# Encoder trunk on one Trainium2 core: the gate's norm divided between two engines, the attention sums copied one step sooner, and a narrower final norm

## The chip, the cores and the metric

The kernel runs on 1 core of one Trainium2 chip. The metric is the device time of one execution, in microseconds (us), smaller is better. The core has five engines that run their own instruction streams and meet at semaphores: TensorE (PE; its weight loads are shown as PEld), VectorE (DVE), ScalarE (ACT), GpSimd (POOL) and SyncE (SP, which here only issues transfers).

## The reference

An encoder of 2 layers over 512 positions of width 1024, all in float32. Each layer has a mixer of two kinds of heads side by side, a cross-attention into 256 memory tokens, and a gated MLP with a convolution of width 3. The change touches the mixer and the final norm. Cut to these:

```python
def rmsnorm(x, g):
    return x * rsqrt(mean(x * x, -1) + EPS) * g

def layernorm(x, g, b):
    xc = x - mean(x, -1)
    return xc * rsqrt(mean(xc * xc, -1) + EPS) * g + b

# mixer, with h = rmsnorm(x, norm_mix_g[l]) and its projection cut in parts
o_mla = softmax(q @ k.T * scale) @ v          # 8 heads, 512 x 512 scores
u, v = gelu(h_u), gelu(h_v)                   # 512 positions x 512 columns each
v = layernorm(v, ln_g, ln_b)                  # "the gate's norm"
o_sg = u * (w_s @ v + b_s)                    # in chunks of 128 positions
x = x + concat(rmsnorm(o_mla, g1), rmsnorm(o_sg, g2)) @ w_out
# ... memory attention, MLP ...
out = rmsnorm(x, final_norm_g)                # after the last layer
```

## The kernel before

Activations live transposed, features on the 128 partitions and the 512 positions along the free dimension: `x` is 8 tiles of 128x512. The gate branch is the other way round: `vt` and `u` are 4 tiles of 128 positions by 512 columns. Every matrix product is three products of reduced-precision halves (`product3`, L1414 to L1416: high with high, low with high, high with low). The high half is a copy by ScalarE, the low half a subtraction by VectorE or GpSimd. Weights arrive in blocks of 128x1024 by transfers that SyncE issues, are rounded by ScalarE (L480) and subtracted by GpSimd (L362).

No scheduler orders the work. The order on each engine is the order of its code, and what an engine waits for is a count of a semaphore (`need`). The mixer is one loop over 8 heads h and 4 query blocks t, i = 4h+t, written once for each engine:

- TensorE, step (h,t): the scores of i+4, the transposes of the exponentials of i (`turn`, L1572), at t = 0 the spreading of the reciprocal sums of head h-1 over 128x512 (`spread_sums`, L1603), at t = 1 and 2 the product with the values (`attend`), at t = 1 of an even head the key projection `k_proj`, at t = 3 a query projection, and at `MIX_STEPS` two groups of the gate's product (`mix`). In head 7 it also turns the gated tiles (`turn_gated`, L1634). `turn(i)` waits for `turned_lo(i-2)`; `k_proj` waits for the copy of the sums; the first `mix` waits for all four low halves of the gate (`svl_done`).
- ScalarE: the exponentials of i+3 (L631), then at t = 1 the copy of the spread sums (`copy_sums`, L647), then the high half of the turned tile (`turned_hi`, L639). Between these, at fixed steps: query and key parts (L614, L618), weight blocks, squares for the variance (L710) and of the gated tiles (L719), small roots (L536, L538), and the high halves of the gate (L726) at `SPLIT_STEPS`.
- VectorE: the row minimum of the scores of i+4 (L1116), at t = 0 a query product (L1093), at t = 3 `attended` (L1128), the low half `turned_lo(i)` (L1142). At `NORM_STEPS` it normalizes one tile of the gate with two linked operations (L1196, L1198), where `link` makes an operation wait for the end of the one before. The small root of the variance (L1016 to L1018) stands ahead of the first.
- GpSimd: the low halves of queries (L375), odd keys (L380) and the gate (L385), the product of the gated tiles with their scale (L417), and the low halves of weight blocks, in one queue.

The end of the program: VectorE adds the last projection to `x` (L1386), ScalarE squares it (L455), VectorE sums seven squares into `acc` (L965), and TensorE multiplies `acc` and the last square by a matrix of ones (L1836, L1838), which puts the column sums on all 128 partitions. Then follow Ln and Exp on 128x512 (L887, L889), the mean square and one Newton step in four operations of VectorE (L985 to L995), and eight output tiles (L1392), each of which SyncE stores as soon as it is there (L338).

## Time and profile before

| | us |
|---|---|
| Median of 3 runs | 1496.52 (1496.45 to 1496.69) |
| The profiled execution | 1496.6 |
| Its span in the profile | 1494.7 |
| TensorE busy | 1456.8 (97%) |
| VectorE busy | 744.2 (50%) |
| ScalarE busy | 698.6 (47%) |
| GpSimd busy | 665.1 (45%) |

The span is what the profiler saw from the first to the last instruction; 1.9 us of the execution lie around it. The mean granted clock of TensorE is 0.995 of its full 2.4 GHz. The busy times say which engine is loaded, not which one waits. For that the views of waits and the timelines of single stretches are read, which stand below. In a timeline the number in brackets at the end of a line is how long the engine was idle before the instruction, and what released it.

### The profile page before, as it was taken

How to read it: one execution, taken by the hardware profiler on the slowest of the kernel's cores; microseconds unless marked ns; L12 is line 12 of the kernel's file. 1: busy time of each engine (PE TensorE's matmuls, PEld its weight loads, DVE VectorE, ACT ScalarE, POOL GpSimd, SP SyncE). 2: the span in 40 equal slices, each digit the busy share in tenths (PEclk: the TensorE clock that was granted, in tenths of full speed). 3: DMA queues.
4: the chain of work that ended last, by engine and by line, in shares of the span. 5: the costliest groups of instructions: out<-in, count | busy, mean ns of one | idle time of the engine just before them, and what ended most of it. 6: DMA issues, size and time to landing. Idle time of an engine off the chain costs nothing.

```text
span 1494.7 us, 19415 instructions
## 1 busy us (share of the span) xinstructions
PE 1456.8 (97%) x6852; PEld 1195.4 (80%) x6852; DVE 744.2 (50%) x1132; ACT 698.6 (47%) x1131; POOL 665.1 (45%) x329
## 2 busy tenths in 40 slices
PE   8998999999999999999999899999999999999996
PEld 7776789888888888888877677888888888888884
DVE  7737678343355420445264676781536544024534
ACT  6576646354354421344355875553534344124432
POOL 2443348644343554354445333684343454435350
PEclk9999999999999999999999999999999999999999
DMA  5320225412133333232323102463131332323231
GB/s 193 113 82 15 71 80 159 144 56 71 59 105 105 112 99 99 85 100 83 117 84 99 57 29 73 125 183 99 29 99 57 113 112 83 114 85 100 78 90 57
DMA packets 38889, 138.75 MB, mean 93 GB/s; under 512 B 4449, under 2 KB 4705, under 8 KB 38561
## 3 DMA queue, kind: packets, MB, share of 16 engines
q1 hardware_dynamic: 37872, 134.25, 29.1%
q10 hardware_dynamic: 944, 3.51, 0.7%
q8 instruction: 49, 0.80, 0.2%
q14 instruction: 24, 0.19, 0.0%
HBM read 135.64 MB, written 2.10 MB: 92 GB/s over the span
## 4 chain that ended last, share of the span: by engine, by line
PE 74%; issue 10%; DVE 6%; ACT 5%; POOL 4%; DMA 0%; SPq 0%; POOLq 0%; DVEq 0%; ACTq 0%
PE ps L1414 24%; PE ps L1416 24%; PE ps L1415 24%; POOL w_lo L362 4%; ACT work L631 1%; DVE small L1116 1%; DVE arena L1142 0%; ACT h_hi L639 0%; DVE work L1196 0%; PE ps L1572 0%; ACT h_hi L710 0%; DMA raw<-blocks_d 0%; DVE work L1128 0%; DVE arena L1277 0%; DVE work L1392 0%
## 5 line engine op out<-in xcount | busy, mean ns | idle before, releaser
L362 POOL TENSOR_TENSOR w_lo<-raw,w_hi 128x1024 fp32r<-128x1024 f32 x244 | 594.3, 2454 | 665.1 <-ACT w_hi L480 665.1
L1414 PE MATMUL ps<-h_hi,w_hi 128*128 128x512 f32 (+1 forms) x1040 | 406.9, 391 | 3.9 <-DVE w_lo L931 2.0
L480 ACT ACTIVATE w_hi<-raw 128x1024 fp32r<-128x1024 f32 x247 | 255.0, 1054 | 329.6 <-PE ps L1416 326.5
L1415 PE MATMUL ps<-h_lo,w_hi 128*128 128x512 f32 (+1 forms) x1040 | 403.8, 388 | 0.0
L1416 PE MATMUL ps<-h_hi,w_lo 128*128 128x512 f32 (+1 forms) x1040 | 403.7, 388 | 0.0
L1414 PE MATMUL ps<-arena,w_hi 128*128 128x512 f32 (+1 forms) x648 | 241.1, 372 | 6.0 <-ACT work L647 5.9
L1416 PE MATMUL ps<-arena,w_lo 128*128 128x512 f32 (+1 forms) x648 | 238.8, 369 | 0.0
L1415 PE MATMUL ps<-arena,w_hi 128*128 128x512 f32 (+1 forms) x648 | 238.6, 368 | 0.0
L1414 PEld LDWEIGHTS ps<-h_hi,w_hi 128*128 128x128 f32 x1040 | 195.7, 188 | 48.7 <-issue 3.5
L1415 PEld LDWEIGHTS ps<-h_lo,w_hi 128*128 128x128 f32 x1040 | 195.6, 188 | 40.5 <-issue 1.0
L1416 PEld LDWEIGHTS ps<-h_hi,w_lo 128*128 128x128 f32 x1040 | 195.7, 188 | 40.3
L1313 DVE TENSOR_TENSOR work<-ps,work 128x512 f32<-128x512 f32 x88 | 54.7, 684 | 216.3 <-PE ps L1416 215.6
L1414 PEld LDWEIGHTS ps<-arena,w_hi 128*128 128x128 f32 x648 | 122.2, 189 | 28.3 <-ACT work L647 7.5
L1227 DVE TENSOR_TENSOR x<-x,ps 128x512 f32<-128x512 f32 x60 | 37.5, 683 | 205.7 <-PE ps L1416 205.7
L1416 PEld LDWEIGHTS ps<-arena,w_lo 128*128 128x128 f32 x648 | 122.2, 189 | 20.5
L1415 PEld LDWEIGHTS ps<-arena,w_hi 128*128 128x128 f32 x648 | 122.3, 189 | 19.4
L846 ACT ACTIVATE work<-work,par 128x512 f32<-128x512 f32 x88 | 64.6, 806 | 110.8 <-DVE work L1313 110.8
L1324 DVE SCALAR_TENSOR_TENSOR work<-work,par 128x511 f32<-128x511 f32 x88 | 66.1, 752 | 12.0 <-DVE work L1321 3.1
L1321 DVE SCALAR_TENSOR_TENSOR work<-work,par 128x511 f32<-128x511 f32 x88 | 69.0, 784 | 0.0
L1116 DVE TENSOR_REDUCE small<-ps 128x1 f32<-128x512 f32 x64 | 43.4, 680 | 40.9 <-PE ps L1416 40.5
L1414 PE MATMUL ps<-arena 128*128 128x512 f32 (+2 forms) x160 | 60.0, 375 | 0.0
L852 ACT ACTIVATE work<-work 128x512 f32<-128x512 f32 x44 | 27.9, 633 | 61.2 <-DVE work L1324 61.2
(190 smaller groups left out, 1803.1 us busy)
## 6 DMA issues: line engine op xcount, KB each, us to landing
raw<-blocks_d SPq DMA_DIRECT2D x247, 512.0 KB, 3.5
work<-memT_d ACTq DMA_DIRECT2D x2, 1024.0 KB, 4.9
outT_d<-work SPq DMA_DIRECT2D x8, 256.0 KB, 2.2
x<-xT_d SPq DMA_DIRECT2D x3, 512.0 KB, 7.7
work<-ln_d ACTq DMA_DIRECT2D x2, 512.0 KB, 3.6
x<-xT_d SPq DMA_DIRECT2D x2, 256.0 KB, 4.6
raw<-blocks_d SPq DMA_DIRECT2D x2, 256.0 KB, 5.1
par<-par_d ACTq DMA_DIRECT2D x2, 113.5 KB, 4.0
```

Of the source, the lines that this page charges most:

```text
L362: gp.tensor_tensor(w_lo[:, b % SPLIT, :], raw[:, b % RAW, :], w_hi[:, b % SPLIT, :].bitcast(F32), ALU.subtract).then_inc(lo_done.sem, 1)
L480: act.activation(w_hi[:, b % SPLIT, :], raw[:, r, :], ACT.Copy).then_inc(hi_done.sem, 1)
L846: act.activation(conv[:, bank + 2 * j + s, :], lin[:, 2 * j + s, :], ACT.Identity, bias=cb, scale=cw).then_inc(tap1.sem, 1)
L852: act.activation(cg, cg, ACT.Silu).then_inc(silu_done.sem, 1)
L1116: dve.tensor_reduce(low_score[:, i % 4:i % 4 + 1], ps[BS[i % 3]][:, :], AXX, ALU.min)\
L1227: dve.tensor_tensor(x[:, t0 + j, :], x[:, t0 + j, :], ps[banks[j]][:, :], ALU.add)\
L1313: dve.tensor_tensor(lin[:, 2 * j + s, :], ps[bank + 2 * s + j][:, :], rs, ALU.mult)\
L1321: dve.scalar_tensor_tensor(out=c[:, 1:SEQ], in0=a[:, 0:SEQ - 1], scalar=col(C_W0 + at), in1=c[:, 1:SEQ], op0=ALU.mult, op1=ALU.add).then_i ...
L1324: dve.scalar_tensor_tensor(out=c[:, 0:SEQ - 1], in0=a[:, 1:SEQ], scalar=col(C_W2 + at), in1=c[:, 0:SEQ - 1], op0=ALU.mult, op1=ALU.add).th ...
L1414: pe.matmul(out, a_hi, b_hi, start=first, stop=False)
L1415: pe.matmul(out, a_hi, b_lo, start=False, stop=False)
L1416: return pe.matmul(out, a_lo, b_hi, start=False, stop=last)
```

## The change

1. The gate's norm. VectorE keeps tiles 2 and 3, at steps (1,2) and (2,1). Tiles 0 and 1 go to GpSimd (`gate_norm`), three operations each, where each waits for the one before: add the negative mean and multiply by the root (a tensor_scalar with two columns), multiply by the gain, add the bias. GpSimd is released by a new signal, `vroot`, which VectorE gives between the small root and its own first norm. ScalarE makes the high halves in the order 2, 0, 3, 1, at (1,3), (2,3), (2,3) and (3,0), and GpSimd the low halves in the same order.
2. ScalarE copies the spread sums of head h-1 at (h,0), behind `turned_hi`, where it did at (h,1), ahead of it.
3. The squares of the gated tiles move from (5,0), (5,1), (5,1), (5,2) to (5,0), (5,2), (5,2), (5,3), and what follows them one step back each: the variance to (5,3), the root to (6,0), its Newton step and the signal to GpSimd to (6,1), one square of the attention output to (6,1) and its addition to (6,2).
4. The final norm. TensorE makes the column sums as 128x4 (four products with one column of ones, for `acc` and for the last square), the root is taken on 128x4 by ScalarE and VectorE as elsewhere in the kernel, and four transposes of a broadcast column spread it over a PSUM bank, twice, into banks 5 and 6. VectorE makes output tiles 2 to 7 straight from bank 5. ScalarE has multiplied tiles 0 and 1 by their gains ahead of time, copies bank 6 to SBUF, and GpSimd multiplies the two.
5. The stores: SyncE issues those of tiles 2, 4, 0, 6, ScalarE those of 3, 5, 1, 7.

The diff, without the new semaphores:

```diff
-NORM_STEPS = ((1, 2), (1, 3), (2, 1), (2, 3))
-SPLIT_STEPS = ((1, 3), (2, 0), (2, 3), (3, 0))
+NORM_STEPS = {(1, 2): 2, (2, 1): 3}
+GP_NORMS = (0, 1)
+SPLIT_STEPS = ((1, 3), (2, 3), (2, 3), (3, 0))
+SPLIT_TILES = (2, 0, 3, 1)
...
-GATED_STEPS = ((5, 0), (5, 1), (5, 1), (5, 2))
-GATED_VAR, GATED_ROOT = (5, 2), (5, 3)
-SCALED_STEP = (6, 0)
-
-SQUARE_STEPS = ((4, 3), (5, 3), (7, 1))
-ADD_STEPS = ((6, 1), (7, 2))
+GATED_STEPS = ((5, 0), (5, 2), (5, 2), (5, 3))
+GATED_VAR, GATED_ROOT = (5, 3), (6, 0)
+SCALED_STEP = (6, 1)
+
+SQUARE_STEPS = ((4, 3), (6, 1), (7, 1))
+ADD_STEPS = ((6, 2), (7, 2))
...
-            for t in range(KD):
-                sp.wait_ge(out_done, t + 1)
+            for t in (2, 4, 0, 6):
+                if t < 2:
+                    sp.wait_ge(out_gp, t + 1)
+                else:
+                    sp.wait_ge(out_done, t - 1)
                 sp.dma_start(out_d[:, t, :], conv[:, t, :]).then_inc(stored, 16)
...
+                def gate_norm(n):
+                    t = GP_NORMS[n]
+                    if n == 0:
+                        need(vroot, 1)
+                        need(ln_in, 16)
+                    gp.tensor_scalar(vt[:, t, :], vt[:, t, :], nmean[:, t:t + 1], sm_t[:, t:t + 1], ALU.add, ALU.mult)\
+                        .then_inc(gn_step.sem, 1)
+                    need(gn_step, 2 * n + 1)
+                    gp.tensor_tensor(vt[:, t, :], vt[:, t, :], ln_gb[:, 0, :], ALU.mult).then_inc(gn_step.sem, 1)
+                    need(gn_step, 2 * n + 2)
+                    gp.tensor_tensor(vt[:, t, :], vt[:, t, :], ln_gb[:, 1, :], ALU.add).then_inc(vn_gp.sem, 1)
...
                 key_low(1)
+                gate_norm(0)
                 gate_low(0)
                 query_low(4)
-                for t in range(1, TT):
-                    gate_low(t)
+                gate_norm(1)
+                for n in range(1, TT):
+                    gate_low(n)
...
+            for t in range(2):
+                gp.wait_ge(gained, t + 1)
+                gp.wait_ge(final_copied, 1)
+                gp.tensor_tensor(conv[:, t, :], conv[:, t, :], rs, ALU.mult).then_inc(out_gp, 1)
...
-                    if t == 1 and h >= 1:
-                        copy_sums(h - 1)
                     turned_hi(i)
+                    if t == 0 and h >= 1:
+                        copy_sums(h - 1)
...
+                if t in (2, 3):
+                    act.activation(conv[:, t - 2, :], x[:, t - 2, :], ACT.Copy,
+                                   scale=mix_g[:, DEPTH * KD + t - 2:DEPTH * KD + t - 1]).then_inc(gained, 1)
-            act.wait_ge(ssq_done.sem, ssq_done.at(DEPTH, 1))
-            act.activation(r0, ps[4][:, :], ACT.Ln, bias=eps, scale=1.0 / D).then_inc(ln_done.sem, 1)
-            act.wait_ge(ln_done.sem, ln_done.at(DEPTH, 1))
-            act.activation(r0, r0, ACT.Exp, scale=-0.5).then_inc(r0_done.sem, 1)
+            act.wait_ge(s_v.sem, s_v.at(DEPTH, 1))
+            act.activation(sm_r, sm_v, ACT.Ln).then_inc(s_ln.sem, 1)
+            act.wait_ge(s_ln.sem, s_ln.at(DEPTH, 1))
+            act.activation(sm_r, sm_r, ACT.Exp, scale=-0.5).then_inc(s_r0.sem, 1)
+            act.wait_ge(final_spread, 2)
+            act.activation(rs, ps[6][:, :], ACT.Copy).then_inc(final_copied, 1)
+            for t in (3, 5, 1, 7):
+                if t < 2:
+                    act.wait_ge(out_gp, t + 1)
+                else:
+                    act.wait_ge(out_done, t - 1)
+                act.dma_start(out_d[:, t, :], conv[:, t, :]).then_inc(stored, 16)
...
-                    if (h, t) == NORM_STEPS[0]:
+                    if (h, t) == min(NORM_STEPS):
                         small_root(1)
+                        dve.sem_inc(vroot.sem, 1)
                         need(ln_in, 16)
...
-            mean_square(MIX, 4)
-            newton(MIX)
-            for t in range(KD):
+            dve.wait_ge(ssq_tok.sem, ssq_tok.at(DEPTH, 1))
+            link(dve.tensor_scalar(sm_v, ps[4][:, 0:TT], 1.0 / D, EPS, ALU.mult, ALU.add))
+            dve.wait_ge(ssq_tok.sem, ssq_tok.at(DEPTH, 2))
+            dve.scalar_tensor_tensor(out=sm_v, in0=ps[7][:, 0:TT], scalar=1.0 / D, in1=sm_v, op0=ALU.mult, op1=ALU.add)\
+                .then_inc(s_v.sem, 1)
+            small_root(0)
+            dve.wait_ge(final_spread, 1)
+            for t in range(2, KD):
                 dve.scalar_tensor_tensor(out=conv[:, t, :], in0=x[:, t, :], scalar=mix_g[:, DEPTH * KD + t:DEPTH * KD + t + 1],
-                                         in1=rs, op0=ALU.mult, op1=ALU.mult).then_inc(out_done, 1)
+                                         in1=ps[5][:, :], op0=ALU.mult, op1=ALU.mult).then_inc(out_done, 1)
...
-            pe.matmul(ps[4][:, :], ones[:, :], acc, start=True, stop=False)
+            for t in range(TT):
+                last = pe.matmul(ps[4][:, t:t + 1], acc[:, P * t:P * t + P], ones[:, 0:1], start=True, stop=True)
+            last.then_inc(ssq_tok.sem, 1)
             pe.wait_ge(sq_done.sem, sq_done.at(DEPTH, KD))
-            pe.matmul(ps[4][:, :], ones[:, :], sq[:, 0, :], start=False, stop=True).then_inc(ssq_done.sem, 1)
+            for t in range(TT):
+                last = pe.matmul(ps[7][:, t:t + 1], sq[:, 0, P * t:P * t + P], ones[:, 0:1], start=True, stop=True)
+            last.then_inc(ssq_tok.sem, 1)
+            pe.wait_ge(dve_step.sem, dve_step.at(DEPTH, 4))
+            for bank in (5, 6):
+                for t in range(TT):
+                    last = pe.transpose(ps[bank][:, P * t:P * t + P], sm_t[:, t:t + 1].to_broadcast([P, P]), ident[:, :])
+                last.then_inc(final_spread, 1)
```

## Rows read from the trace of the kernel before

**Rows 1.** The page: busy time of engines, chain that ended last.
```profile
PE 1456.8 (97%) x6852; PEld 1195.4 (80%) x6852; DVE 744.2 (50%) x1132; ACT 698.6 (47%) x1131; POOL 665.1 (45%) x329
...
PE 74%; issue 10%; DVE 6%; ACT 5%; POOL 4%; DMA 0%; SPq 0%; POOLq 0%; DVEq 0%; ACTq 0%
```

**Rows 2.** TensorE's waits, 826:918 us: total, times, longest us.
```profile
PE ps L1414 <- ACT work L647: 3.0, 1, 3.0
PE ps L1572 <- DVE h_lo L1142: 2.1, 3, 1.6
```

**Rows 3.** Timeline of TensorE, layer two: start, us, line, what, count, idle before.
```profile
849.33 0.63 PE L1572 MATMUL ps<-ident,work 128*128 128x128 f32 x4 [1.62 <-DVE h_lo L1142]
...
854.32 0.50 PE L1414 MATMUL ps<-arena,w_hi 128*128 128x512 f32 x1 [2.98 <-ACT work L647]
...
867.00 0.36 PE L1414 MATMUL ps<-h_hi,w_hi 128*128 128x256 f32 x1
...
901.29 0.60 PE L1634 MATMUL ps<-ident,work 128*128 128x128 f32 x4
902.48 0.30 PE L1572 MATMUL ps<-ident,work 128*128 128x128 f32 x1 [0.60 <-DVE arena L1142]
```

**Rows 4.** Timeline of VectorE in the same loop.
```profile
845.86 0.75 DVE L1196 SCALAR_TENSOR_TENSOR work<-work,small 128x512 f32<-128x512 f32 x1
...
848.51 0.67 DVE L1142 TENSOR_TENSOR h_lo<-ps,h_hi 128x512 fp32r<-128x512 f32 x1
...
851.25 0.68 DVE L1093 TENSOR_TENSOR work<-ps,turn_q 128x512 f32<-128x512 f32 x1
...
860.72 1.63 DVE L1196 SCALAR_TENSOR_TENSOR work<-work,small 128x512 f32<-128x512 f32 x1
...
896.47 0.69 DVE L1116 TENSOR_REDUCE small<-ps 128x1 f32<-128x512 f32 x1 [0.15 <-DVE small L1018]
...
897.67 1.37 DVE L1136 TENSOR_TENSOR work<-work 128x512 f32<-128x512 f32 x1
```

**Rows 5.** Timeline of ScalarE in the same loop.
```profile
847.43 0.63 ACT L726 ACTIVATE h_hi<-work 128x512 fp32r<-128x512 f32 x1 [1.70 <-DVE work L1198]
...
851.97 0.63 ACT L614 ACTIVATE arena<-work 128x512 fp32r<-128x512 f32 x1 [2.67 <-DVE work L1093]
...
853.69 0.58 ACT L647 ACTIVATE work<-ps 64x512 f32<-64x512 f32 x1
```

**Rows 6.** Timeline of GpSimd in the same loop.
```profile
848.14 1.27 POOL L385 TENSOR_TENSOR h_lo<-work,h_hi 128x512 fp32r<-128x512 f32 x1 [3.71 <-ACT h_hi L726]
...
860.52 1.28 POOL L385 TENSOR_TENSOR h_lo<-work,h_hi 128x512 fp32r<-128x512 f32 x1 [5.35 <-ACT h_hi L726]
...
896.45 4.49 POOL L417 TENSOR_TENSOR work<-work,small 128x512 f32<-128x512 f32 x4 [3.75 <-DVEq L1208]
```

**Rows 7.** Line L417 of GpSimd in the whole span: duration ns, min/median/max.
```profile
L417 POOL TENSOR_TENSOR work<-work,small x8: 1035/1041/1491, 164.5 to 899.9; 128x512 f32<-128x512 f32 x8
```

**Rows 8.** Timeline of the tail, all engines.
```profile
1481.07 1.12 PE L1836 MATMUL ps<-work,ones 128*128 128x512 f32 x2 [1.77 <-DVE work L965]
...
1486.66 5.39 DVE L1392 SCALAR_TENSOR_TENSOR work<-x,mix_g,work 128x512 f32<-128x512 f32 x8
1487.44 4.97 SPq L338 DMA_DIRECT2D outT_d<-work  x8
```

**Rows 9.** Timelines elsewhere: column sums and small roots on 128x4.
```profile
991.61 0.95 PE L1431 MATMUL ps<-ones,work 128*128 128x1 f32 x8
...
993.83 0.21 ACT L536 ACTIVATE small<-small 128x4 f32<-128x4 f32 x1
...
845.29 0.13 DVE L1016 TENSOR_TENSOR small<-small 128x4 f32<-128x4 f32 x1
```

**Rows 10.** Transfers, 1480:1495 us, in 40 slices: busy tenths, GB/s.
```profile
DMA  0000000000000000000000899999999999998000
GB/s 0 0 0 0 0 0 0 0 0 0 0 0 0 0 0 0 0 0 0 0 0 0 339 377 366 404 366 377 393 382 371 393 377 372 404 361 311 0 0 0
```

29 lines of the change are left out of this document (19 added, 10 removed).

## The prediction

> **What bounds the kernel now.** I read the page's busy shares first: TensorE is busy for 1456.8 us, 97% of the span,, and the chain that ended last runs over it for 74% [rows 1]. So only two things can pay: a stretch where TensorE waits, and the end, where it has nothing left to do. The waits of TensorE in the attention loop of the second layer show the first kind: 2.98 us for ACT's L647 (the copy of the sums; the view rounds it to 3.0), 2.1 us for VectorE's L1142 (turned_lo), and smaller ones [rows 2]. Layer one repeats the loop 732 us earlier with the same waits within 0.3 us, so each gain there counts twice. The timeline names the places [rows 3]. I call a pass of the loop (h,t), its number i = 4h+t. The transposes of (2,1) start at 849.33 after 1.62 us of idle. The key projection of (2,1) starts at 854.32, after 2.98 us.
>
> VectorE explains both [rows 4]. At 845.86 it starts the first norm pair (L1196, L1198), at (1,2). The next pair follows at (1,3). Between the two, turned_lo(7) starts at 848.51, and TensorE's transposes at 849.33 need it. The query product of (2,0) (L1093) is late too, at 851.25. ACT waits 1.70 us for the first pair, then 2.67 us for that product, and only then reaches the split, one exponential and the copy of the sums at 853.69 [rows 5]. The copy is late because of what stands before it in ACT's order.
>
> The second kind is the tail [rows 8]: from the last column sums at 1481.07 to the first output tile at 1486.66 nothing overlaps but single 128x512 operations; then eight tiles follow in 5.39 us and eight stores.
>
> **What GpSimd costs VectorE.** GpSimd started L385 at 860.52 for 1.28 us, and VectorE's L1196, started at 860.72, took 1.63 us instead of 0.75 [rows 4, 6]. It ended 0.55 us after GpSimd did: it was blocked, not slowed. The same in the gated stretch: beside L417's four products an add took 1.37 us [rows 4, 6], where the same form is 0.7 us elsewhere; GpSimd's own products rose from 1.04 to 1.49 us there [rows 7]. An operation of VectorE with one input from PSUM isn't blocked: turned_lo started at 848.51, inside GpSimd's L385 of 848.14, and took its usual 0.67 us. The Trainium skill, "SBUF — State Buffer", section "Who interferes with whom", states it as a rule: a VectorE instruction with two SBUF inputs and a GpSimd instruction that reads SBUF exclude each other for the whole instruction. The trace agrees with the numbers above, and the rule speaks against this change.
>
> **Part 1, norm divided and sums one step sooner, per layer.** Removed: VectorE's pairs at (1,3) and (2,3); the second of these cost 1.63+0.75 = 2.4 us [rows 4]. The pairs left are tile 2 at (1,2) and tile 3 at (2,1). Added: GpSimd does tiles 0 and 1 in three operations each, one tensor_scalar and two products. The trace shows no tensor_scalar on GpSimd; the nearest rows are its products, 1.04 us with a column operand and 1.28 with a full one [rows 6, 7]. I take 1.1. The Trainium skill, "GPSIMD Engine Reference", section "Engine selection", says that one-input work runs on GpSimd at about line rate, which would make it some 0.6 us; by it, each layer would gain 0.5 us more. The sum goes by the rows.
>
> After the small root, VectorE signals GpSimd and goes on with its own pair. The same signal before L417 shows how close that is: after the last small operation GpSimd started at 896.45, VectorE at 896.47 [rows 4, 6]. I take VectorE as first for L1196; then the tensor_scalar comes between L1196 and L1198, which wait for each other, and L1198 is blocked. The pair grows by 1.1 us, and what VectorE has queued behind it (reduce, attended(0), turned_lo(7)) moves by as much. TensorE's transposes start at 849.33+1.1 = 850.4.
>
> ACT then splits tile 2 at 848.5 (before: 847.43), does an exponential (0.7) and turned_hi (0.5), and copies the sums at about 850.2, since the copy now stands in (2,0), and its input comes with the transposes of (2,0), long before. TensorE reaches the key projection at 850.4 + 0.38 (transposes) + six products of 0.23 = 852.2, and no wait is left: 854.3-852.2 = 2.1 us. Without the block it would be 3.2; with GpSimd first, both operations of the pair are blocked and it is about 1.0.
>
> What is late next: tile 3's pair on VectorE. By then GpSimd has finished gate_norm(0) (about 846.7 to 851), gate_low of tile 2 and query_low(4) (to 853.6), and is in gate_norm(1), to about 858.4. Both operations of the pair (from 854.0) can be blocked, 3.1 us in place of 1.5. That puts turned_lo(11) at about 860.2 and holds the transposes of (3,1) at 861.0, where TensorE alone would be at 860.4. So of the 2.1 us 1.5 are kept. The two splits of (2,3) lie on ACT beside the pair that VectorE no longer has; the last one, tile 1 at (3,0), is done at 864.1, its GpSimd low part at 864.9, and the first mixing product (before: at 867.0 [rows 3]) wants it at 865.5: covered by 0.6 us. query_low(5) and key_low(2) stand behind it in GpSimd's queue and are due at (4,0), some 3.5 us later; the weight lows behind them are not due before the loop's end. **1.5 us per layer; from 0 to 3.5.**
>
> **Part 2, gated squares spread, per layer.** ACT has one square less before turned_hi(22), so the transposes of (6,0) and (6,1) come 1.2 us sooner by ACT. But the root moves a step back, from (6,0) to (6,1). Everything from there hangs on VectorE and GpSimd: the scale is ready at about 897.1 where it was 896.3, GpSimd's four products take 4.49 us [rows 6], so the turning of the gate (L1634, at 901.29 before [rows 3]) waits until 901.8. The 0.60 us wait at 902.48 [rows 3] was for a turned_lo that now comes 0.7 us sooner; behind the later turning it can use 0.3. **0.3 us per layer, from -0.6 to 1.2.** Copying the sums sooner costs nothing in the other heads: ACT does the same work, and the input is there 0.6 us after the transposes.
>
> **Part 3, the tail.** Before: 1481.07 to 1486.66, 5.59 us [rows 8]. After: four products with one column took 0.95 us, twice [rows 9], the second batch with no start-up, 0.8: 1482.9. One more 128x4 operation 0.15, Ln and Exp 0.24 each: 1483.5. Three small linked operations at 0.19 (0.13 to 0.16 busy [rows 9]): 1484.1. Four transposes, 0.60 [rows 3], with hand-overs: 1485.0, a gain of 1.6. Then six tiles on VectorE in place of eight, spaced 0.66 (5.39 less one duration over seven): 4.05 us in place of 5.39. GpSimd's two start after the second four transposes (0.4) and ACT's copy (0.6) and end after 1.2+2×1.28 = 3.7 us, inside that. VectorE reads the scale from PSUM, so it isn't blocked. ACT's gains for tiles 0 and 1 fall into the last projection's time, where it waits for x. The stores set what of these 1.34 us remains. Before, the first was issued 0.8 us after its tile began, data flowed 0.8 us later for some 15 slices of 0.375 us, 5.6 us, with the transfer engines 90% busy or more in all but the ends, and 0.8 us passed after the last [rows 8, 10]: 8.0 us. Fed faster they can gain about a tenth: 0.8+0.8+5.1+0.8 = 7.5 us. If they kept pace with the tiles it would be 4.05+2.65 = 6.7. I take 7.5, nearest to the row: a gain of 0.5. On SP, tile 0's store stands ahead of tile 6's; GpSimd has tile 0 at 2.5 and tile 6 is due at 3.4, so nothing queues. **2.1 us, from 1.3 to 3.0.**
>
> Sum: 2×1.5 + 2×0.3 + 2.1 = 5.7 us. The profiled execution took 1496.6 us (span 1494.7 and 1.9 around it), which is the median 1496.52 within 0.1. 1496.6-5.7 = 1490.9.
>
> **Rivals.** (a) The block hardly bites: a short tensor_scalar, or VectorE's second operation slips in. [...] 2×(3.2+0.3)+2.1 = 9.1, 1487.5. (b) GpSimd gets in first, and all four operations of the two pairs are blocked: part 1 gives 0.4 per layer, 2×0.7+2.1 = 3.5, 1493.1. For it: 896.45 against 896.47. (c) The waits only change place, to the first mixing product or the turning of the gate, which now hang on a longer GpSimd chain: the layers give nothing, only the tail does: 1494.5. For it: margins of 0.6 us and a scale that is later than before. (d) Slower: a tensor_scalar with two column operands on GpSimd is much longer than its products. VectorE's pair, then the transposes, wait for each whole one; it decides from about 1.1+5.7/2 = 4.0 us for one, and at 5.5 us the time is 1496.6-5.7+2×4.4 = 1499.7. Against: no GpSimd row of this size is above 1.5 us. (e) The change doesn't do at the end what it says: two issuing engines share the same transfers, which are at their limit, and the faster tiles give nothing, the tail 1.6 alone: 1491.4. The Trainium skill, "DMA: Bandwidth & Descriptors", section "Issuing engines are not separate DMA queues", says just this; the trace has stores from one engine only and can't show it.
>
> **How the numbers follow.** Forecast 0.38 (with (e) in it 0.45), (a) 0.20, (b) 0.18, (c) 0.12, (d) 0.05. The likeliest gives 1490.9. The range goes from (a) to (c): 1487.5 to 1494.5, and leaves out what lies beyond both and (d), 2 in 10. A measurement of this kernel tells about 0.2% from no change, 3 us: under 1493.5 is faster. That takes in the forecast, (e), (a) and four fifths of (b): 0.80. Same is (c), the rest of (b): 0.16. Slower: 0.04, most of (d).
>
> **What would show it.** Right: TensorE's wait for L647 gone in both layers; its wait for turned_lo at (2,1) up from 1.6 to about 2.7; L1198 or L1196 of the first pair near 1.9 us; the turning of the gate waiting for GpSimd's L417 products; first output tile 3.9 us after the last column sums start; the last six tiles within 4.1 us. Wrong: pairs at 0.75 each (then (a)), a GpSimd tensor_scalar over 2 us (then (d)), or a wait at the first mixing product (then (c)).

## The result, and the profile after

The changed kernel takes 1486.26 us in the median of five executions, against 1496.52 before: a ratio of 0.9933, with a 95% interval of 0.9919 to 0.9948. One of the five was disturbed and took 4026.71 us; the other four lie between 1485.62 and 1488.40, with a median of 1486.06, and the ratio is theirs. The gain is 10.3 us where 5.7 were forecast, and the time lies 1.2 us below the low end of the range. The profiled execution took 1485.62 us with a span of 1483.8, which is 11.0 us less than the profiled execution of before.

The page of the changed kernel, busy time and the chain that ended last:

```profile
PE 1455.2 (98%) x6872; PEld 1198.1 (81%) x6872; DVE 734.9 (50%) x1123; ACT 698.3 (47%) x1134; POOL 683.9 (46%) x343
...
PE 78%; issue 9%; DVE 4%; POOL 4%; ACT 4%; DMA 0%; SPq 0%; POOLq 0%; DVEq 0%; ACTq 0%
```

TensorE's share of the chain that ended last rises from 74% to 78% [rows 1]: less of that chain now passes over other engines. Its waits in the attention loop of layer two (820 to 912 us; total, times, longest):

```profile
PE ps L1619 <- DVE h_lo L1183: 2.1, 1, 2.1
PE ps L1681 <- POOL work L442: 1.8, 1, 1.8
```

Two waits of more than 0.2 us are left, the same in layer one. The wait for the copy of the sums, 3.0 us in [rows 2], is gone, and so are the small ones; one for GpSimd ahead of the gated transposes is new. TensorE's timeline in that loop (L1619 is the turning of an exponential's tile, L1650 the spreading of the sums, L1681 the turning of the gate):

```profile
844.09 0.63 PE L1619 MATMUL ps<-ident,work 128*128 128x128 f32 x4 [2.07 <-DVE h_lo L1183]
...
852.78 0.60 PE L1650 MATMUL ps<-ident,small 128*64 128x128 f32 x4
854.22 0.63 PE L1619 MATMUL ps<-ident,work 128*128 128x128 f32 x4
...
892.25 0.66 PE L1681 MATMUL ps<-ident,work 128*128 128x128 f32 x4 [1.75 <-POOL work L442]
```

VectorE in the same loop (L1238 and L1240 are the norm pair, L1183 is turned_lo):

```profile
840.30 0.75 DVE L1238 SCALAR_TENSOR_TENSOR work<-work,small 128x512 f32<-128x512 f32 x1 [0.16 <-DVE small L1059]
841.09 1.06 DVE L1240 SCALAR_TENSOR_TENSOR work<-work,small 128x512 f32<-128x512 f32 x1
...
847.60 0.87 DVE L1238 SCALAR_TENSOR_TENSOR work<-work,small 128x512 f32<-128x512 f32 x1
848.51 1.67 DVE L1240 SCALAR_TENSOR_TENSOR work<-work,small 128x512 f32<-128x512 f32 x1
```

GpSimd in the same loop (L400, L403 and L405 are its three norm operations, L442 its products for the gate):

```profile
840.30 1.31 POOL L400 TENSOR_SCALAR work<-work,small 128x512 f32<-128x512 f32 x1 [1.55 <-DVEq L1234]
841.70 1.58 POOL L403 TENSOR_TENSOR work<-work 128x512 f32<-128x512 f32 x1
...
847.16 0.77 POOL L400 TENSOR_SCALAR work<-work,small 128x512 f32<-128x512 f32 x1
...
887.71 4.48 POOL L442 TENSOR_TENSOR work<-work,small 128x512 f32<-128x512 f32 x4 [4.84 <-DVEq L1250]
```

Both engines started at 840.30. VectorE's first operation took its usual 0.75 us and GpSimd's tensor_scalar 1.31 instead of the 0.77 that it takes at 847.16, where it began 0.44 us ahead of VectorE's operation; then VectorE's second took 1.06. The pair ended 1.85 us after it began, against 1.54 for two free ones.

The tail, and the transfers from 1468.9 to 1483.9 us in 40 slices (GB/s):

```profile
1471.24 1.05 PE L1884 MATMUL ps<-ones,work 128*128 128x1 f32 x8 [1.77 <-DVE work L1006]
...
1472.15 1.03 PE L1888 MATMUL ps<-ones,work 128*128 128x1 f32 x8
...
1474.58 1.97 PE L1893 MATMUL ps<-ident,small 128*128 128x128 f32 x8 [1.40 <-DVE small L1059]
1475.81 4.04 DVE L1439 SCALAR_TENSOR_TENSOR work<-x,mix_g,ps 128x512 f32<-128x512 f32 x6 [1.29 <-PE ps L1893]
...
1476.59 2.96 SPq L350 DMA_DIRECT2D outT_d<-work  x4
...
GB/s 0 0 0 0 0 0 0 0 0 0 0 0 0 0 0 0 0 0 0 0 0 275 380 375 380 381 363 392 380 386 381 381 386 369 380 381 369 35 0 0
```

The first output tile starts 4.57 us after the column sums (before 5.59 [rows 8]), the six tiles take 4.04 us, and 7.99 us pass from the first tile to the end of the span (before 8.04). The transfers flow at about the same 380 GB/s as in [rows 10].

**Four stages.** I cut each profiled execution at three starts that all kernels have: the first transposes of the attention loop of layer one, of layer two, and the first column sums of the tail. Before: 94.90, 828.10 and 1481.07 us of a span of 1494.7; after: 94.59, 822.44 and 1471.24 of 1483.8. The spans are printed to 0.1 us, so the tail column is good to 0.05. In us (the last column names the places where TensorE ran at the lower clock ahead of the tail; S is the start, 12 to 24 us, 1 and 2 the attention loop of a layer):

| kernel | start | layer one | layer two | tail | lower clock |
|---|---|---|---|---|---|
| before | 94.90 | 733.20 | 652.97 | 13.63 | S, 1 |
| after | 94.59 | 727.85 | 648.80 | 12.56 | S |
| tail_only | 93.06 | 731.96 | 654.16 | 14.02 | 2 |
| copy_only | 93.62 | 730.01 | 651.06 | 13.61 | |
| norm_only | 93.84 | 729.92 | 650.86 | 13.58 | |
| norm_copy | 93.05 | 728.97 | 650.02 | 13.56 | 1, 2 |
| kept_busy | 92.75 | 731.97 | 652.94 | 13.64 | |
| act_scales | 94.52 | 727.63 | 649.90 | 14.15 | S, 2 |
| late_signal | 95.38 | 727.30 | 648.29 | 13.43 | S |
| one_queue | 92.97 | 729.14 | 648.85 | 12.54 | 1 |
| filled_before | 93.27 | 731.96 | 652.97 | 13.60 | |
| filled_no_gated | 92.94 | 727.81 | 648.77 | 12.08 | |
| filled_after | 93.30 | 727.90 | 648.81 | 12.09 | |
| filled_late | 93.15 | 727.40 | 648.35 | 13.10 | |

Between before and after: 0.31 at the start, 5.35 in layer one, 4.17 in layer two, 1.07 in the tail, 10.9 us. The layers do the same work with the same waits, so the 1.2 us between 5.35 and 4.17 wanted an explanation of its own, and got one: the clock. Stretches of the kernel before (windows: the length, the busy time of PE, PEld, DVE, ACT and POOL, and behind them the granted clock, the busy share of the transfer engines and GB/s):

```profile
118.00:122.00 4.00, 1.03 (x5) 0.76 (x5) 2.35 (x5) 2.78 (x6) 2.50 (x2) 1.00 0.00 0
122.00:126.00 4.00, 4.00 (x14) 2.72 (x13) 3.56 (x7) 3.82 (x7) 0.00 (x0) 0.57 0.00 0
```

And its matmuls there:

```profile
122.21 0.63 PE L1415 MATMUL ps<-arena 128*128 128x512 f32 x1
122.63 0.63 PE L1416 MATMUL ps<-arena 128*128 128x512 f32 x1
...
125.56 0.40 PE L1415 MATMUL ps<-h_lo,arena 128*64 128x512 f32 x1
125.79 0.40 PE L1416 MATMUL ps<-h_hi,arena 128*64 128x512 f32 x1
```

At (2,1) of layer one TensorE was busy for 1.03 of 4 us (118 to 122), and for most of the next 4 us it ran at 0.57 of the clock, that is mostly at 1.2 instead of 2.4 GHz: matmuls 0.42 us apart, then 0.23 again. In layer two the same waits left it at 1.00. The changed kernel has its wait at (2,1) earlier, up to 116.25 us, and kept the clock there and behind it:

```profile
114.00:118.00 4.00, 1.94 (x11) 1.31 (x11) 4.00 (x8) 3.00 (x7) 3.92 (x3) 1.00 0.02 4
118.00:122.00 4.00, 4.00 (x22) 2.95 (x21) 3.31 (x4) 3.95 (x9) 3.83 (x5) 1.00 0.01 2
```

### The profile page after: what moved, and what is told of

Read it like the earlier page. It is cut to its first block, busy times and chain, and to the rows that moved or that the text cites. A ratio compares the mean times of both kernels' runs of the same rounds, so it can differ in the third digit from the quotient of the medians.

```text
span 1483.8 us, 19468 instructions
## 1 busy us (share of the span) xinstructions
PE 1455.2 (98%) x6872; PEld 1198.1 (81%) x6872; DVE 734.9 (50%) x1123; ACT 698.3 (47%) x1134; POOL 683.9 (46%) x343
## 4 chain that ended last, share of the span: by engine, by line
PE 78%; issue 9%; DVE 4%; POOL 4%; ACT 4%; DMA 0%; SPq 0%; POOLq 0%; DVEq 0%; ACTq 0%
PE ps L1461 25%; PE ps L1463 25%; PE ps L1462 25%; POOL w_lo L374 4%; PE ps L1619 1%; ACT work L660 1%; POOL work L442 1%; DVE small L1157 0%; DVE arena L1183 0%; DMA raw<-blocks_d 0%; DVE arena L1319 0%; ACT arena L668 0%; DVE work L1006 0%; ACT arena L633 0%; PE ps L1471 0%
```

## The experiments

Each label stands for one kernel. All runs stand beside runs of the kernel before on the same chip, with medians of 1496.33, 1496.24 and 1496.18 us in the three sets of four kernels.

**The three parts alone.** The first set undoes or does one part each.

tail_only is the changed kernel with the layers of before:

```diff
-NORM_STEPS = {(1, 2): 2, (2, 1): 3}
-GP_NORMS = (0, 1)
+NORM_STEPS = {(1, 2): 0, (1, 3): 1, (2, 1): 2, (2, 3): 3}
+GP_NORMS = ()
...
-GATED_VAR, GATED_ROOT = (5, 3), (6, 0)
+GATED_VAR, GATED_ROOT = (5, 2), (5, 3)
...
-                    if t == 0 and h >= 1:
+                    if t == 1 and h >= 1:
                         copy_sums(h - 1)
```

> The kernel before with the new final norm and the stores from two engines alone; the layers as before. Theory (the trace after): the stretch from the last column sums to the end shrinks from 13.6 to 12.6 us, all of it ahead of the first output tile, since the stores already flowed at some 380 GB/s before: 1495.4 us. Rival (as predicted): faster tiles also shorten the stores, 2.1 us in all: 1494.4.

Measured: 1495.59 us (1493.85 to 1496.87, ten runs), ratio 0.9997 [0.9987, 1.0006]. The number fits the theory by accident: the theory wanted a tail of 12.6 us, and the stage table has 14.02, 0.4 more than before. Its timeline shows why:

```profile
1479.18 1.67 PE L1881 MATMUL ps<-ones,work 128*128 128x1 f32 x8 [1.77 <-DVE work L1004]
1480.72 1.84 PE L1885 MATMUL ps<-ones,work 128*128 128x1 f32 x8
1483.96 1.97 PE L1890 MATMUL ps<-ident,small 128*128 128x128 f32 x8 [1.40 <-DVE small L1057]
```

The column sums took 1.67 and 1.84 us where after has 1.05 and 1.03; the granted clock from 1480 to 1482 was 0.50. Each sum is four one-column products, which the trace records as eight, and what they cost is the loading of weights: the eight loads of the first sum were busy for 1.58 us here and for 0.97 in after. The form of before, one product of 512 columns for each sum at 1.12 and 1.02 us [rows 8], ran ahead of the fall in every profile here (tail 13.56 to 13.64). How much of its gain the new tail keeps depends on where the clock falls. From the first column sum to the first output tile it takes 4.57 us where the fall comes behind the sums (after, one_queue), 5.16 and 5.39 where it comes during them (act_scales, late_signal), and 6.00 here, where it came 0.25 us into them; before took 5.59. From the first tile to the end it is 8.0 us in every profile but that of act_scales, where it is 9.0 and the stores landed late for a cause that no run shows.

copy_only is the kernel before with copy_sums(h - 1) behind turned_hi at t == 0 instead of ahead of it at t == 1:

```diff
-                    if t == 1 and h >= 1:
-                        copy_sums(h - 1)
                     turned_hi(i)
+                    if t == 0 and h >= 1:
+                        copy_sums(h - 1)
```

> The kernel before with the sums copied at (h,0) instead of (h,1), nothing else. Theory: TensorE's wait of 2.98 us for the copy goes in both layers, but VectorE still has four norm pairs, so turned_lo of (2,3) and (3,0) is late next and takes back all but 0.7 to 1.5 us per layer; the clock's 1.6 us come on top if the wait that is left is short enough: 1492 to 1495. Rival: the copy was the whole matter and the norm's division gives nothing: 1489, the same as with both.

Measured: 1490.22 us (1489.95 to 1491.97, seven runs), ratio 0.9966 [0.9955, 0.9978]. TensorE's waits in layer two:

```profile
PE ps L1572 <- DVE h_lo L1142: 2.7, 3, 1.6
PE ps L1572 <- DVE arena L1142: 1.3, 3, 0.6
```

The wait for the copy is gone whole, and the stage table gives 1.95 and 1.91 us a layer. The time lies below the range of the theory, and yet its mechanism is there: counted from the start of the loop, the transposes of (2,2) are 3.15 us sooner than before and those of (3,2) only 0.91, since three waits for VectorE of 0.3, 0.3 and 0.9 us have come up between them. What the theory missed is the 1.0 us that comes back behind that, up to (6,0). The rival, that the norm's division gives nothing on top, falls with norm_copy below.

norm_only is the kernel before with the norm divided and nothing else:

```diff
-NORM_STEPS = ((1, 2), (1, 3), (2, 1), (2, 3))
-SPLIT_STEPS = ((1, 3), (2, 0), (2, 3), (3, 0))
+NORM_STEPS = {(1, 2): 2, (2, 1): 3}
+GP_NORMS = (0, 1)
+SPLIT_STEPS = ((1, 3), (2, 3), (2, 3), (3, 0))
+SPLIT_TILES = (2, 0, 3, 1)
```

> The kernel before with the norm divided alone; the copy of the sums at (h,1). Theory: ACT gets to the copy some 2 us sooner since its input from VectorE is sooner, TensorE's wait for it falls from 2.98 to between 0.6 and 1.1 us: 2x2+1.6 = 5.6 us, about 1491. Rival (the lock on the shared port decides): VectorE's pair beside GpSimd is longer, ACT comes no sooner, within 1 us of before: 1496.

Measured: 1490.01 us (1489.08 to 1491.14, five runs), ratio 0.9963 [0.9949, 0.9977]. Its waits:

```profile
PE ps L1596 <- DVE h_lo L1165: 2.3, 2, 2.1
PE ps L1596 <- DVE arena L1165: 0.9, 2, 0.6
PE ps L1438 <- ACT work L669: 0.9, 1, 0.9
```

The wait for the copy falls from 3.0 to 0.9 us, as the theory had it, and the stage table gives 2.04 and 2.11 us a layer. The rival is wrong.

norm_copy joins the two, with the tail and the gated steps of before:

```diff
-NORM_STEPS = ((1, 2), (1, 3), (2, 1), (2, 3))
+NORM_STEPS = {(1, 2): 2, (2, 1): 3}
...
-                    if t == 1 and h >= 1:
+                    if t == 0 and h >= 1:
                         copy_sums(h - 1)
```

> Norm divided and sums copied one step sooner; gated squares and final norm as before. Theory: TensorE's waits at (2,1) fall by 2.5 us per layer, the one at the spreading of the sums in (4,0) of 0.55 goes too, and in layer one the clock no longer falls, 1.6 us more: 2x3.1+1.6 = 7.8 us, 1488.7. Rival (as predicted): 1.5 per layer, since VectorE's blocked pairs take the rest back: 1493.5.

Measured: 1487.34 us (1486.44 to 1488.31, four runs), ratio 0.9943 [0.9926, 0.9960]. That is below the theory's 1488.7, and the rival's 1493.5 is excluded. Its profile has the lower clock in both layers, so the theory's 1.6 us for a clock that no longer falls was not borne out. With the price of such a fall from the stage table (1.24 in layer one, before against tail_only; 1.2 in layer two, tail_only against before) its layers are 727.7 and 648.8, which is 4.2 us a layer where 3.1 were expected. filled_no_gated below, which has the same layers and no fall in them, has 727.81 and 648.77. The two parts add up within 0.2 us: 1.95 + 2.04 and 1.91 + 2.11.

**The clock alone.** kept_busy is the kernel before with matmuls that nothing uses in TensorE's waits at (2,1):

```diff
+                def busy(n):
+                    for _ in range(n):
+                        pe.matmul(ps[B_PV][64:128, 0:P], ones[:, 0:64], ones[:, :], start=True, stop=True)
...
                 def k_proj(p):
+                    if p == 2:
+                        busy(12)
...
+                    if (h, t) == (2, 1):
+                        busy(6)
                     turn(i)
```

> The kernel before with work added that nothing uses: six matmuls of 128x128 ahead of the transposes of step (2,1) and twelve ahead of k_proj(2), all in time that TensorE spends waiting (3.0 us and 2.1 us in the layer loops before). Theory (the clock is a term of its own: after those waits TensorE runs some 3 us at the lower of its two clocks, in layer one or two or both of an execution, as in the stretch 122 to 126 us of the kernel before, at 0.57, where each such stretch costs about 1.5 us): no stretch near 122 or 852 us is below 1.00, the waits lose at most what the added work fills, the later steps start as before, and the median falls from about 1496.3 to 1494.5 (1494.2 to 1495.0), with the executions closer together. Rival (the time follows the lengths of the waits alone, and the lower clock costs nothing that a later wait doesn't take back): 1496.3, or 0.5 more where the added matmuls run past the end of a wait.

Measured: 1495.08 us (1493.20 to 1495.72, eleven runs), ratio 0.9991 [0.9982, 1.0000]. No stretch of the layers is under 1.00 and the layers take 731.97 and 652.94 us, as long as where they ran at the full clock without it (731.96 in tail_only, 652.97 in before), so this work in a wait cost nothing. But the median is just above the theory's range, and the executions did not come closer together: five lie at 1493.2 to 1493.9 and six at 1495.1 to 1495.7. A third place was left, which the windows of several kernels show at the start; here of before and then of after:

```profile
16.00:20.00 4.00, 4.00 (x11) 3.13 (x12) 3.78 (x7) 3.42 (x5) 0.00 (x0) 0.57 0.45 141
```

```profile
16.00:20.00 4.00, 4.00 (x13) 3.09 (x13) 3.77 (x7) 3.42 (x6) 0.00 (x0) 0.63 0.41 135
```

Both come after a wait of 2.0 and 1.8 us for the second block of weights. Profiles with such a stretch have a start of 94.5 to 95.4 us, those without one of 92.8 to 93.8. filled_before fills that wait too, in project, on top of kept_busy's fills (eleven instead of twelve ahead of k_proj(2)):

```diff
+                        if l == 0 and b0 == B_LAT and n_kp == 1:
+                            busy(7, 3)
                         block_ready(b0 + n_kp, i, step)
```

> The kernel before with matmuls that nothing uses in the three places where TensorE has waited and then shows the lower clock in one execution or another: seven in the 2.0 us wait at 13.9 us (layer one's first transfers), and in each layer six ahead of the transposes of (2,1) and eleven ahead of k_proj(2). Theory (each fall costs about 1.5 to 1.8 us and is drawn anew in each execution; the steps of 1.5 us between executions of one kernel are these falls and nothing else): no stretch before 1480 us below 0.99, one cluster of times at 1493.3 (1492.8 to 1493.8). Rival (the steps have another cause, since with the layers' waits filled the executions still fell into 1493.2 to 1493.9 and 1495.1 to 1495.7): still two clusters, the median near 1495.1.

Measured: 1493.86 us (1493.35 to 1495.82, eleven runs), ratio 0.9988 [0.9979, 0.9997]. Windows of its profile:

```profile
16.00:20.00 4.00, 4.00 (x18) 3.29 (x19) 3.77 (x7) 3.42 (x6) 0.00 (x0) 1.00 0.46 135
118.00:122.00 4.00, 3.55 (x23) 2.79 (x22) 2.31 (x4) 3.38 (x8) 2.36 (x2) 1.00 0.00 0
122.00:126.00 4.00, 4.00 (x21) 3.08 (x20) 3.94 (x9) 4.00 (x9) 0.30 (x1) 1.00 0.01 2
```

Nine of eleven executions are within 1 us now, at 1493.35 to 1494.31. Two, at 1495.26 and 1495.82 with a mean clock of 0.996 instead of 0.997 or 0.998, seem by that clock to have had a fall still, which no profile here places. So the theory holds for most of the spread, not for all of it. The fills lower the median of the kernel before by 2.3 us.

**What the change is worth without the clock.** filled_after is the changed kernel with fills in five waits:

```diff
+                        if l == 0 and b0 == B_LAT and n_kp == 1:
+                            busy(7, 3)
...
                     if f == 0:
+                        busy(6, B_PV)
                         need(sg_normed, 4)
...
+                    if (h, t) == (2, 1):
+                        busy(7, B_PV)
...
+            pe.wait_ge(add_done.sem, add_done.at(DEPTH, 1))
+            busy(6, 4)
             pe.wait_ge(add_done.sem, add_done.at(DEPTH, KD - 2))
...
+            busy(5, 3)
             pe.wait_ge(dve_step.sem, dve_step.at(DEPTH, 4))
```

> The changed kernel with the same matmuls at the start (seven), ahead of (2,1) (seven) and ahead of the gated transposes (six), and in the tail ahead of the column sums (six) and ahead of the transposes that spread the root (five). Theory: 1485.6 has one fall, at the start; without it 1484.0, and with the tail's transposes of the root at the higher clock (0.6 instead of 1.23 us) 1483.4 (1482.9 to 1484.0), in one cluster. The difference to the kernel before with its waits filled is then what the change is worth without the clock: 9.3 to 9.9 us, of which 1.7 in the tail, so some 4.0 a layer. Rival (the extra over the forecast of 5.7 us was mostly the clock): no more than 7.5 us between the two.

Measured: 1484.15 us (1483.88 to 1485.08, five runs), ratio 0.9925 [0.9911, 0.9939]. Against filled_before that is 9.7 us, in the medians and in the spans (1491.8 and 1482.1). The median is 0.15 us above the range that was expected. The stages place the 9.7 us: 4.06 and 4.16 in the layers, 1.51 in the tail. So of the 10.3 us of the measured gain at least nine are work and waits; the rival that most of the surplus was the clock is wrong. Its tail:

```profile
1470.01 1.05 PE L1895 MATMUL ps<-ones,work 128*128 128x1 f32 x8 [0.32 <-DVE work L1006]
1470.92 1.03 PE L1899 MATMUL ps<-ones,work 128*128 128x1 f32 x8
...
1473.36 1.09 PE L1905 MATMUL ps<-ident,small 128*128 128x128 f32 x8 [0.16 <-DVE small L1059]
1474.12 4.04 DVE L1439 SCALAR_TENSOR_TENSOR work<-x,mix_g,ps 128x512 f32<-128x512 f32 x6 [0.82 <-PE ps L1905]
```

The transposes of the root take 0.76 us up to the first tile instead of 1.23, and the first tile comes 4.11 us after the sums began, 1.5 sooner than before.

**The gated squares.** filled_no_gated is filled_after with these steps of before, and without the fill ahead of the gated transposes:

```diff
-GATED_STEPS = ((5, 0), (5, 2), (5, 2), (5, 3))
-GATED_VAR, GATED_ROOT = (5, 3), (6, 0)
-SCALED_STEP = (6, 1)
+GATED_STEPS = ((5, 0), (5, 1), (5, 1), (5, 2))
+GATED_VAR, GATED_ROOT = (5, 2), (5, 3)
+SCALED_STEP = (6, 0)
```

> As the changed kernel with its waits filled, but the gated squares, their variance, root and the fourth pair's tiles at the steps that they had before (no fill ahead of the gated transposes). Theory (spreading them takes away waits of 0.28 and 0.66 us in each layer and adds 1.2 us ahead of the gated transposes less what the engines had queued: 0.3 to 0.45 a layer): 0.6 to 0.9 slower, 1484.2. Rival (what goes at (5,x) comes back whole ahead of the gated transposes): within 0.2 of it, 1483.4.

Measured: 1484.67 us (1483.44 to 1485.10, five runs), ratio 0.9928 [0.9914, 0.9941]. The medians, 0.5 us apart with executions up to 1.7 us apart, don't decide between the two, but the stages do: they differ by 0.09 and 0.04 us a layer, the spread form being the slower. The theory missed and the rival is right. Its waits in layer two:

```profile
PE ps L1625 <- ACT work L660: 0.7, 1, 0.7
PE ps L1625 <- DVE arena L1183: 0.6, 1, 0.6
PE ps L1625 <- DVE h_lo L1183: 0.4, 1, 0.4
```

The 0.7 and 0.6 us are what spreading takes away (the 0.4 is what the fill leaves of the wait at (2,1)). Counted from the start of the loop, the spread form is 0.86 us ahead at (6,1) and 1.1 ahead at the spreading of the sums in (7,0), and its gated transposes then start 0.8 later (69.80 us against 68.98) and its end 0.1 later. This part moved two waits into one and gave nothing.

act_scales asks whether that one wait can be had back: ScalarE makes the gate's products of tiles 2 and 3, at (6,2) and (6,3).

```diff
-                for t in range(TT):
+                for t in range(2):
...
+                    if (h, t) in ((6, 2), (6, 3)):
+                        g = t
+                        need(gated_root, 1)
+                        act.activation(u[:, g, :], u[:, g, :], ACT.Copy, scale=sm_t[:, g:g + 1]).then_inc(sg_normed.sem, 1)
```

> The changed kernel, with the scale products of gated tiles 2 and 3 on ScalarE at steps (6,2) and (6,3) and only tiles 0 and 1 left to GpSimd (two of 1.12 us instead of four). Theory (the 1.8 us for which TensorE waits ahead of the gated transposes is GpSimd's four products and nothing else is late there): the wait falls to under 0.5 us in both layers, 1.3 us a layer, and the whole to 1483.7 (1483.2 to 1484.5) from about 1486.2. Rival (ScalarE's two operations of 0.7 us hold its copies of the transposes, so that the wait comes back ahead of the head steps (7,0) and (7,1)): 1485.8 to 1486.8.

Measured: 1486.10 us (1485.70 to 1488.01, five runs), ratio 0.9933 [0.9919, 0.9947], the same as the changed kernel. Its waits in layer one:

```profile
PE ps L1623 <- DVE h_lo L1187: 2.1, 1, 2.1
PE ps L1685 <- ACT work L753: 1.0, 1, 1.0
PE ps L1623 <- DVE arena L1187: 0.4, 1, 0.4
```

The wait falls from 1.8 to 1.0 us and now ends with ScalarE, whose product of tile 3 stands behind an exponential and a copy; 0.4 us comes back one step on. Layer one gains 0.2 us, and layer two, less a fall of 1.2, 0.1. The rival is right.

**The block of the first pair.** late_signal starts GpSimd only when VectorE has ended its pair:

```diff
-                        dve.sem_inc(vroot.sem, 1)
...
+                        if (h, t) == min(NORM_STEPS):
+                            need(vn_done, 1)
+                            dve.sem_inc(vroot.sem, 1)
```

> The changed kernel, with GpSimd started on its first norm only when VectorE has ended its own first pair. Theory (GpSimd's tensor_scalar holds VectorE's first pair by about 0.5 us and by no more): VectorE's pair takes 1.45 us instead of 1.9, the 2.1 us wait ahead of the transposes of (2,1) falls to about 1.6, and in two layers the kernel gains 1.0 at most: 1485.2. GpSimd's six operations then end some 1.5 us later (853 instead of 851.4 in layer two), which costs nothing if the splits behind them have slack. Rival (they have none, so that the splits or GpSimd's low parts of the value blocks come late): 1486.3 to 1488.5. By the prediction's figure of 1.1 us for the block the gain would have been 2.2 us: 1484.0.

Measured: 1484.63 us (1483.63 to 1486.16, four runs), ratio 0.9921 [0.9906, 0.9937]. VectorE's pair and GpSimd's first operation:

```profile
840.41 0.75 DVE L1237 SCALAR_TENSOR_TENSOR work<-work,small 128x512 f32<-128x512 f32 x1
841.20 0.75 DVE L1239 SCALAR_TENSOR_TENSOR work<-work,small 128x512 f32<-128x512 f32 x1
```

```profile
842.11 0.77 POOL L400 TENSOR_SCALAR work<-work,small 128x512 f32<-128x512 f32 x1 [3.12 <-DVEq L1243]
```

Two free operations, and the layers are 0.55 and 0.51 us shorter than after's, which is the theory. The median alone couldn't say so: it lies between the theory's 1485.2 and the 1484.0 of a block of 1.1 us, in executions up to 2.5 us apart. The gain comes in two pieces: the transposes of (2,1) are 0.2 us sooner, and the 1.44 us from 852.78 to 854.22 in the changed kernel, from the spreading of the sums to the transposes of (3,1), become 1.14, so that this was a hold of 0.3. GpSimd's norm ended 0.8 us later without harm, and a block of 1.1 us, the prediction's figure, is excluded by the stages and by the pair itself, 1.85 us against 1.54.

filled_late is late_signal with all of filled_after's fills (one of them shown):

```diff
-                        dve.sem_inc(vroot.sem, 1)
...
+                        if (h, t) == min(NORM_STEPS):
+                            need(vn_done, 1)
+                            dve.sem_inc(vroot.sem, 1)
...
+                    if (h, t) == (2, 1):
+                        busy(7, B_PV)
...
```

> As the changed kernel with its waits filled, with GpSimd started behind VectorE's own first pair. Theory (the wait ahead of the transposes of (2,1) is 0.2 us shorter in each layer, and nothing later takes it back): 0.3 to 0.5 faster, 1483.0, and the fastest of all. Rival (GpSimd's norm and splits, now 0.8 to 1.3 us later, hold something): the same or up to 0.5 slower.

Measured: 1483.77 us (1482.70 to 1484.89, five runs), ratio 0.9921 [0.9907, 0.9934]. The layers are 0.50 and 0.46 us shorter than filled_after's, as the theory had it, and the medians are 0.4 us apart. In the profiled execution the tail is 1.0 us longer, since here the clock fell during the last fills:

```profile
1470.78 2.03 PE L1453 MATMUL ps<-ones 128*64 128x128 f32 x10
```

The same five fills took 1.31 us in filled_after. Here they ran past the end of VectorE's root, so that the transposes began 0.5 us late, and these again took 1.24 us up to the first tile. A fill is free only as long as it ends within the wait, and at the lower clock it may not. filled_late has the lowest median of all; against late_signal alone, 0.9 us above it, four and five runs don't settle the order.

**The queue of the stores.** one_queue issues all eight stores from SyncE:

```diff
-            for t in (2, 4, 0, 6):
+            for t in (2, 3, 4, 0, 5, 6, 1, 7):
```

> The changed kernel with all eight stores issued by SyncE, in the order in which the tiles end. Theory (from the first output tile on the end is set by the transfers' flow, about 380 GB/s over all sixteen engines, and not by who issues them): 1486.2, within 0.3. Rival (issues from one engine follow one another too slowly, and the second issuing engine brought what there is of the gain behind the first tile): 0.5 later, 1486.7 or more.

Measured: 1486.08 us (1484.05 to 1488.52, four runs), ratio 0.9936 [0.9921, 0.9951]. The tail takes 12.54 us, against 12.56 with two issuing engines:

```profile
1475.53 4.04 DVE L1433 SCALAR_TENSOR_TENSOR work<-x,mix_g,ps 128x512 f32<-128x512 f32 x6 [1.29 <-PE ps L1887]
1476.31 4.48 SPq L350 DMA_DIRECT2D outT_d<-work  x8
```

The theory holds: the second issuing engine brings nothing. The Trainium skill, "DMA: Bandwidth & Descriptors", section "Issuing engines are not separate DMA queues", says as much, and these two runs agree within 0.02 us.

## Why the prediction was wrong

The direction was right and the size was not. By its own terms, without the clock: part 1 was to give 1.5 us a layer and gave 4.2; part 2 0.3 and gave nothing (-0.1); part 3 2.1 and gave 1.07 (1.5 with the clock held). Two layers make 8.3 and the tail 1.1, together 9.4; with 1.2 of a fall that only the profile of before had in its layers and 0.3 at the start that is the 10.9 us of the spans.

**Part 1, the block at (2,1): mis-sized.** The step took the unseen tensor_scalar at 1.1 us, from the nearest products of GpSimd, and let the pair grow by the whole of it. Free it takes 0.77 us, and the pair grew by 0.3. The transposes of (2,1) came 0.4 us later than in before, counted from the start of the loop, not 1.1; the other 0.1 is VectorE standing idle for 0.16 us behind the signal to GpSimd, ahead of its first operation, a term that the prediction doesn't have. late_signal puts the price of the whole encounter at 0.5 us a layer. The Trainium skill's sentence on one-input work ("GPSIMD Engine Reference", section "Engine selection") was nearer than the rows I went by: about 0.6 us by an estimate from it, 0.77 measured. That the two engines exclude each other is borne out: tile 3's second operation, begun at 848.51 beside a product of GpSimd, took 1.67 us and ended 0.55 us after that product, as the operation in the prediction did. But its first was held for 0.1 us only, so the later pair cost 2.5 us where 3.1 were forecast.

**Part 1, what is late next: mis-sized.** The prediction took 0.6 us off for transposes of (3,1) held by tile 3's pair. The hold is there, 0.3 us.

**Part 1, the work removed: the step that failed most.** The pair removed at (2,3) was named, with its 2.4 us, and then priced at nothing, because only the 3.0 us wait for the copy was followed to its end. The sooner copies of the other heads were put at no cost and no gain. From the starts of the transposes, counted from the first of the loop: at (2,2) the changed kernel is 2.8 us ahead (27.71 against 24.88), at the spreading of the sums in (4,0), six passes on, 3.65 (45.00 against 41.35), at the end of the loop 4.1. Between lie the passes (3,2) and (3,3) of 3.40 and 3.48 us that became 3.26 each, a wait of 0.54 us for VectorE at (4,0) and one of 0.28 at (6,0). Nothing in the view of the longest wait shows them; the sum over the loop does.

The account in the place of the forecast's 2.1 - 0.6 = 1.5 is 2.8 at (2,2), 0.3 lost at (3,1), 0.5 regained by (3,3), 0.6 at (4,0), 0.1 by (4,2) and 0.4 at (6,0): 4.1 us. So 1.6 us a layer lie behind (3,1), where the forecast had nothing, 0.7 are more than forecast at (2,2), and 0.3 are a smaller hold. The single runs tell whose the 1.6 us are. norm_only regains 0.9 us behind (3,1), all of it up to (4,1). copy_only regains 1.0 behind (3,2), and the 0.4 at (6,0) is in it, in both layers, while norm_only still has the 0.28 us wait there: that piece belongs to the sooner copy and not to VectorE's backlog. Rival (a), "the block hardly bites", was the right story for the block and stopped at 3.2 us for the same reason.

**Part 2: one side right, and the sum not.** The root moves back a step and the turning of the gate waits for GpSimd's four products: forecast and shown, 1.8 us. The working has the turning 0.5 us later and 0.3 to be had from the 0.60 us wait behind it, and books only the 0.3. Measured against filled_no_gated, the turning starts 0.8 us later, the wait behind it goes, and 0.1 us is lost.

**Part 3: the parts up to the first tile right at full clock, the rest not.** Forecast were 3.9 us from the sums to the first tile; 4.11 were measured with the clock held, 4.57 without, since the transposes that were put at the higher clock run at 0.52 of it. The forecast's 1.6 us became 1.0. The six tiles took 4.04 us (forecast 4.05), but the 0.5 us given to the stores were 0.05 at most: rival (e), shown by the flow of 380 GB/s in both kernels and by one_queue.

**The clock: not in the prediction at all.** The profile of before held the stretch at 122 us with a clock of 0.57. I had compared the waits of the two layers and not their lengths; 733.2 us from loop to loop in layer one couldn't be checked against layer two, but the windows could have been read.

**Its signs and its chances.** Of the signs of being right, the wait for the copy that is gone, the wait for GpSimd at the turning of the gate and the six tiles within 4.1 us came true. The wait at (2,1) is 2.1 us and not 2.7, the longer operation of the first pair 1.06 and not 1.9, the first tile comes after 4.57 us and not 3.9. The forecast and its rivals have chances of 0.93 together; the 0.80 for a faster kernel takes in the 0.07 that no story has.

What is still open: which fall the two late executions of filled_before had, and how often the clock falls at (2,1) in each kernel. The changed kernel has one wait there instead of two (2.1 us instead of 1.6 and 3.0), yet profiles with the divided norm and the sooner copy show a fall there in one_queue, act_scales and, twice, norm_copy. So it isn't shown that the change makes falls rarer.

## What to carry to other kernels

Work taken off an engine with a backlog pays at the small waits behind it too, and not only at the longest: price a removal by the whole stretch until the engine has caught up. When two things are changed at once, a run of each alone says whose a gain is: here the two gave 2.0 us each, and the wait at (6,0) went with the part that seemed to have nothing to do with it. Where an operation has no row, the nearest row may be of another kind (here two inputs against one); take the range from it, not the value. Read the granted clock by stretches before comparing two kernels to within 0.2%, and cut both traces at common starts: that turned one difference of 11 us into terms that repeat to 0.1 us. A shortened tail on TensorE is only as short as its clock allows: the form with many small products came to its first tile after 4.1 us with the clock held and after 6.0 with the clock down from the start, against 5.6 for the form of before, which no run shows at the lower clock.

## What the runs showed of the hardware

Ahead of the tail TensorE's clock fell in three places, each after a wait or two of 1.6 to 3 us, in some profiles and not in others, and in the same kernel in layer one and not in layer two (before; the other way round in act_scales): a fall costs 1.2 us in the attention loops and about 1.6 at the start, and the times of one kernel lie in steps (kept_busy: 1493.2 to 1493.9 and 1495.1 to 1495.7). With matmuls that nothing uses in the waits, the clock was 1.00 in the layers of all five such profiles and in the start of the four that have them there, at no cost in the stages (731.97 and 731.96 us against 731.96). Four of the nine profiles without them have no fall in the layers either, so a profile alone proves little; the narrower times of filled_before go the same way.

A GpSimd tensor_scalar with two column operands on 128x512 took 0.77 us alone and 1.31 against VectorE. Where both started within the same 10 ns, in both layers, VectorE's first operation took its usual 0.75 us, and the loss was shared: 0.5 us on GpSimd, 0.3 on VectorE's second.

Column sums of four tiles as one-column products, recorded as eight, cost 1.05 us at the higher clock and 1.67 to 1.84 where the clock was down for most or all of them.
